# Gate and up products of two layers by seven half products

## The reference

```python
def modulate(x, g, shift, scale):
    return rmsnorm(x, g) * (1.0 + scale) + shift

def swiglu(h, wg, wu, wd):
    return (jax.nn.silu(h @ wg) * (h @ wu)) @ wd

x = x + g2 * swiglu(modulate(x, n_ffn, sh2, sc2), wg, wu, wd)
```

## Time and profile before

| | |
|---|---|
| time, median of 3 runs | 2484.01 us (2483.6 to 2484.45) |
| span of the profiled execution | 2480.8 us |
| its own time | not given apart; the median lies 3.2 us above the span |
| busy: TensorE, weight loads | 97%, 76% |
| busy: VectorE, ScalarE, GpSimd | 38%, 36%, 34% |
| layer 0's feed-forward | about 440 to 1000 us of the span |
| layer 1's feed-forward | about 1433 to 1797 us |

### The profile page before, as it was taken

One profiled execution on the slowest core, in us unless ns is written; L12 is line 12 of the kernel. 1 busy time (PEld: TensorE's weight loads), 2 busy tenths in 40 slices (PEclk: granted clock), 3 DMA queues, 4 the chain that ended last, 5 costly groups with the idle time before them and its releaser, 6 DMA issues.

```text
span 2480.8 us, 34754 instructions
## 1 busy us (share of the span) xinstructions
PE 2402.4 (97%) x13237; PEld 1892.2 (76%) x13237; DVE 941.1 (38%) x1440; ACT 887.4 (36%) x1690; POOL 852.9 (34%) x705
## 2 busy tenths in 40 slices
PE   6999999999999999899899999999999998999998
PEld 4776666788888888687577778888887656888887
DVE  5556632411111113555357331111527666422322
ACT  4336632321121122343556332222423564422331
POOL 1223002223323233352002345445644532444443
PEclk9999999999999999999899999999999999999999
DMA  8630027322222213421020243333333201333332
GB/s 268 187 111 10 2 90 239 89 67 60 62 65 59 68 53 108 122 68 37 7 44 18 86 120 100 93 101 94 103 93 79 80 1 35 94 102 94 98 98 76
DMA packets 336116, 209.76 MB, mean 85 GB/s; under 512 B 29315, under 2 KB 308588, under 8 KB 335986
## 3 DMA queue, kind: packets, MB, share of 16 engines
q1 hardware_dynamic: 333330, 201.98, 28.1%
q10 hardware_dynamic: 2592, 5.96, 0.7%
q0 software_dynamic: 64, 0.04, 0.0%
HBM read 205.82 MB, written 2.12 MB: 84 GB/s over the span
## 4 chain that ended last, share of the span: by engine, by line
PE 86%; DVE 4%; issue 4%; ACT 2%; DMA 1%; POOL 1%; SPq 0%; DVEq 0%; ACTq 0%; POOLq 0%
PE G L1670 22%; PE G L1671 21%; PE G L1672 21%; PE G L1889 5%; PE G L1917 4%; PE G L1902 4%; PE G L1754 1%; POOL wlo L961 1%; PE G L1861 1%; PE G L1935 1%; PE G L1694 1%; PE G L1712 1%; PE G L1695 1%; PE G L1696 1%; DVE ssq L2189 1%
## 5 line engine op out<-in xcount | busy, mean ns | idle before, releaser
L961 POOL TENSOR_TENSOR wlo<-raw,whi 128x512 fp32r<-128x512 f32 x564 | 745.9, 1344 | 1386.6 <-ACT whi L1155 1386.5
L1155 ACT ACTIVATE whi<-raw 128x512 fp32r<-128x512 f32 x564 | 325.4, 624 | 1199.8 <-PE G L1672 1081.4
L1670 PE MATMUL G<-big_a,whi 128*128 128x512 f32 x2016 | 740.3, 367 | 2.2 <-POOL wlo L961 1.5
L1671 PE MATMUL G<-big_a,wlo 128*128 128x512 f32 x2016 | 728.1, 361 | 0.0
L1672 PE MATMUL G<-big_a,whi 128*128 128x512 f32 x2016 | 724.5, 359 | 0.0
L1670 PEld LDWEIGHTS G<-big_a,whi 128*128 128x128 f32 x2016 | 379.9, 188 | 76.3 <-issue 12.6
L1671 PEld LDWEIGHTS G<-big_a,wlo 128*128 128x128 f32 x2016 | 379.8, 188 | 63.3 <-issue 6.7
L1672 PEld LDWEIGHTS G<-big_a,whi 128*128 128x128 f32 x2016 | 378.8, 188 | 60.2
L1670 PE MATMUL G<-big_b,whi 128*128 128x512 f32 x856 | 315.3, 368 | 0.9 <-issue 0.9
L1671 PE MATMUL G<-big_b,wlo 128*128 128x512 f32 x856 | 315.5, 369 | 0.0
L1672 PE MATMUL G<-big_b,whi 128*128 128x512 f32 x856 | 314.3, 367 | 0.0
(11 more groups left out here) (270 smaller groups left out, 2215.2 us busy)
## 6 DMA issues: line engine op xcount, KB each, us to landing
raw<-in_l_ada_w_dram SPq DMA_DIRECT2D x84, 512.0 KB, 4.8
raw<-in_l_ffn_w_gate_dram SPq DMA_DIRECT2D x44, 512.0 KB, 3.8
raw<-in_l_ffn_w_up_dram SPq DMA_DIRECT2D x44, 512.0 KB, 3.8
raw<-in_l_ffn_w_down_dram SPq DMA_DIRECT2D x32, 512.0 KB, 4.0
raw<-in_w_up_dram SPq DMA_DIRECT2D x32, 512.0 KB, 4.0
raw<-in_w_down_dram SPq DMA_DIRECT2D x32, 512.0 KB, 4.0
raw<-in_w_in_dram SPq DMA_DIRECT2D x28, 512.0 KB, 3.8
raw<-in_l_w_in_dram SPq DMA_DIRECT2D x24, 512.0 KB, 4.0
```

Source lines behind the costliest of these rows:

```text
L961: ins = pool.tensor_tensor(wlo[:, u % 2, k:k + 4], raw[:, r % RING, k:k + 4], whi[:, u % 2, k:k + 4].bitcast(F32), ALU.subtract)
L1155: act.activation(whi[:, u % 2, k:k + 4], raw[:, r % RING, k:k + 4], ACT.Copy).then_inc(hi_done, 1)
L1670: pe.matmul(o, whi[:, u % 2, k], rlo[:, k, t0:t0 + w], start=k == order[0], stop=False)
L1671: pe.matmul(o, wlo[:, u % 2, k], rhi[:, k, t0:t0 + w], start=False, stop=False)
```

## The change

With the weights of two output tiles and all input tiles seen as 2 x 2 blocks (input tiles even and odd, output tiles first and second), and the activations as 2 x 2 blocks (input tiles even and odd, tokens first and second half), the two tiles are formed by seven products of half size in place of eight (Winograd's form of Strassen's scheme). Each half product is 4 input tiles by three matmuls over half of the tokens: 384 columns in layer 0, 256 in layer 1.

```diff
+FFN_CHUNKS0 = [(0, 2)] + [(2 + f0, nf) for f0, nf in split_width(FFN // P - 2, 4)]
+LOW_WORDS = T + 2 * TX + 2 * T + 5 * T
...
             for c, (f0, nf) in enumerate(chunks):
-                for i in range(nf * (2 if gated else 1)):
+                plain = nf * (2 if gated else 1)
+                if l in FAST:
+                    plain = 4 if c == 0 else 0
+                for i in range(plain):
                     plan_unit(("up", l, c, i), r=rings[i] if c == 0 and i < len(rings) else None)
+                if l in FAST and nf > plain // 2:
+                    plan_section(l, c, plain // 2, nf - plain // 2)
...
+        FAST = (0,1)
+        CHUNKS = {0: FFN_CHUNKS0 if 0 in FAST else FFN_CHUNKS, 1: FFN_CHUNKS}
```

In both layers tiles 0 and 1 stay plain (4 units). The other 20 are made in sections: layer 0's chunks are now 2, 4, 4, 4, 4, 4 tiles, layer 1's stay 8, 8, 6. A section is a row of sets, gate and up in turn for each pair of tiles. TensorE's part:

```diff
+                for at, st in enumerate(sec["sets"]):
...
+                    for q in range(7):
+                        s = slot_of(sec, 7 * p + q)
+                        if q in (2, 3):
+                            pe.wait_ge(PH["fast", "lod"], 2 * p + q - 1)
+                        elif q >= 5:
+                            r = st["r"][q - 5]
+                            pe.wait_ge(raw_free[r % RING], r // RING + 1)
+                        else:
+                            pe.wait_ge(PH["fast", "lop"], 3 * p + (q + 1 if q < 2 else 3))
...
+                        for j in range(4):
...
+                            xhi, xlo = operands(q, j)
+                            pe.matmul(outs[q], half_slot(whi, s)[:, j], xlo, start=j == 0, stop=False)
+                            pe.matmul(outs[q], half_slot(wlo, s)[:, j], xhi, start=False, stop=False)
+                            mm = pe.matmul(outs[q], half_slot(whi, s)[:, j], xhi, start=False, stop=j == 3)
+                        mm.then_inc(done, 1)
```

`whi` and `wlo` are used as four half slots, so ScalarE can turn out the weights of half product i + 4 when i has finished (`fast_next`). The four sums of weight blocks (`fast_sum`) and the low parts of half products 2 and 3 (`fast_lower`) are VectorE's; the other five low parts are GpSimd's (`fast_lowers`). VectorE also combines the seven results out of PSUM and multiplies gate and up:

```diff
+                    for q in range(7):
+                        if q == 2:
+                            dve.wait_ge(done, 7 * p + 3)
+                            dve.wait_ge(PH["fast", "copy"], p + 1)
+                            dve.tensor_tensor(c[:, 0:2], b26, twice(s1), ALU.add).then_inc(out, 1)
+                        elif q == 4:
...
+                            dve.tensor_tensor(mid, b57, twice(c[:, 1]), ALU.add).then_inc(out, 1)
...
+                            dve.tensor_tensor(c[:, 3], b57[:, 1], mid[:, 0], ALU.add).then_inc(out, 1)
+                            if up:
...
+                                dve.tensor_tensor(c[:, 0::3], c[:, 0::3], sg[:, 0::3], ALU.mult).then_inc(mult, 1)
+                        elif q == 6:
...
+                            dve.tensor_tensor(c[:, 1:3], b34, mid, ALU.add).then_inc(out, 1)
...
+                        if ahead:
+                            if q in (2, 3):
+                                fast_sum(ahead, q - 2)
+                            elif q == 5:
+                                fast_sum(ahead, 2)
+                                fast_lower(sec, ahead, 2)
+                            elif q == 6:
+                                fast_lower(sec, ahead, 3)
+                                fast_sum(ahead, 3)
+                        if not up and at and q < 2:
+                            hidden_tile(sec["sets"][at - 1], q)
```

The activations need four sums too, for each half of the input tiles (`fast_operand_sums`, 8 operations, then 8 high parts on ScalarE and 8 low parts on VectorE). To form them the norm keeps the unrounded tile: ScalarE writes it (`full_row`) and rounds it by a second copy. In layer 1 the sums stand right behind the norm, ahead of the modulation columns; in layer 0 they stand behind them:

```diff
+                if l in FAST and l:
+                    fast_operand_sums(l)
                 if i in HOSTED:
                     ada_columns(*HOSTED[i][1])
```

More of the change, by code:

```diff
@@ L284, in build, with half_tiles, wslot @@
         plan = {}
-        cnt = {"r": 0, "u": 0, "g": 0, "a": 0}
+        cnt = {"r": 0, "u": 0, "g": 0, "a": 0, "p": 0, "pair": 0, "w4": None}
+        flips = []
+        narrow = {}
+        def half_tiles(u):
+            return narrow.get(u, 4)
+        def wslot(u):
+            return (u + sum(1 for first in flips if u >= first)) % 2
         ring_dmas = []
@@ L723, in build @@
         shared_sems(("ffn_act", "ffn_prod", "ffn_hi", "ffn_lo"),
-                    [(f"ffn{i}", (n // P,) * 4) for i, n in enumerate((FFN, FFN, FF2))])
+                    [(f"ffn{i}", ((2 if i in FAST else n // P),) * 2 + (n // P,) * 2)
+                     for i, n in enumerate((FFN, FFN, FF2))])
+        stage_sems("fast", "sum", "hi", "lop", "lod", "done", "copy", "out", "silu", "hid", "full", "tsum", "thi", "tlo")
+        flat_scr = scr[:].rearrange("p a b -> p (a b)")
+        W1, W2, W4 = (part(flat_scr, 3072 + 512 * i, 4, P) for i in range(3))
@@ L1113, in _ @@
                 lower(u)
[L1114 to L1115 removed]
+            for u in range(4):
+                lower(first["up", 0, 0, 0] + u)
+            fast_ffn(0, CHUNKS[0])
+            for u in range(first["down", 0, len(CHUNKS[0]) - 1, 0], first["in1"] + 6):
                 lower(u)
@@ new lines, in fast_ffn @@
+            def fast_ffn(l, chunks, ranges, h_ready):
+                for c, (f0, nf) in enumerate(chunks):
+                    if c == 0:
+                        first_units([("up", l, 0, 0), ("up", l, 0, 1)], lambda b: ranges, h_ready)
+                        ada_turn(*HOSTED[1 + 2 * l][1])
+                        for b in range(2, 4):
+                            unit(("up", l, 0, b), hhi, hlo, ranges)
+                    p = None
+                    if sets_of(l, c):
+                        fast_section(plan["sec", l, c])
+                        p = sets_of(l, c)[-1]["p"]
+                        pe.wait_ge(PH["fast", "copy"], p + 1)
+                    down_pair(l, c, nf, f0, ranges, p)
+                    groups = ADA_DOWN0 if l == 0 and c == len(chunks) - 1 else ()
+                    for b in range(1, KD):
+                        if b > 1:
+                            if p is not None and b < 4:
+                                pe.wait_ge(PH["fast", "out"], 4 * p + b + 1)
+                            unit(("down", l, c, b), ahi, alo, ranges, k_tiles=nf)
+                            if b <= len(groups) and groups[b - 1]:
+                                ada_turn(*groups[b - 1])
+                        if b < len(groups) and groups[b]:
+                            ada(*groups[b])
```

437 lines of the change are left out of this document (409 added, 28 removed).

## The result

The changed kernel takes 2455.02 us (median of 4 runs, 2453.43 to 2459.95), the kernel before beside it 2484.23 us (2483.6 to 2484.45): ratio 0.9886, 95% interval 0.9872 to 0.9900. The forecast was 2448, range 2428 to 2474: faster, as said, and 7 us less of it than said.

What follows compares the result with a forecast made beforehand. TensorE, busy 97% of the span, was taken as the bound. Layer 0's sets -44, layer 1's -4.6 and +13 on the path gave -35.6: span about 2445, forecast 2448 with 3.2 us median offset, range 2428 to 2474.

Steps and rivals of the forecast that it cites:

- Layer 0's sets: Layer 0 gate and up: 84 matmuls per tile pair at 0.174 us, 14.6 us, saving 44 us over 20 sets.
- The rival of weight loads: Weight loads of 0.188 us don't hide behind narrow matmuls; 15.8 us a set in both layers, 2575 us; chance 0.02.
- First chunk: Layer 0's first two-tile chunk: TensorE waits for VectorE's sums, conversions and the second hidden tile; 5 us, bounds 2 to 8.
- Five section ends in layer 0: Layer 0's five later chunks end with a 4.2 us chain against 4.2 us of input tiles; 0.3 each, 1.5 us.
- Modulation loads in the last chunk: Layer 0's last chunk: down units end closer together, so the fourth modulation load comes late; 2.5 us, bounds 0 to 4.
- Layer 1's sets: Layer 1 gate and up: VectorE, with waiting on GpSimd, becomes the bound at 10.65 us a set; 4.6 us saved over 20.
- the opening: Layer 1's first section waits for the first hidden tiles while VectorE carries extra sums and low parts; 2.5 us, 0 to 5.
- the signs named: Expected: layer 1 sets of 10.6 us, gaps before half products 2, 3 or 0 released by VectorE or GpSimd low parts.
- Down units in layer 1: Units 0 and 1 end 1.36 us apart but the third needs 0.62 + 1.27 us; 0.5 us a chunk, 1.5 in all.
- The norms: One more copy a tile (0.8 us) on ScalarE, its turn 2.1 us, hidden behind TensorE's 2.1 us a tile; no cost.
- the waiting stays hidden: Rival: layer 1's sets take TensorE's 10.1 us with no waiting showing, 2437 us; chance 0.19.
- The exclusion costs in full: Rival: VectorE and GpSimd SBUF operations exclude each other whole; layer 1 sets take 11.9 us, 2473 us; chance 0.17.

Runs made afterwards that it cites:

- experiment 5: Changed kernel with layer 0's first chunk reordered (second half of activation sums converted later, tile 0 of both down units first): 2450.62 us; with layer 0 alone by half products, 2449.72.
- experiment 6: Changed kernel with the modulation columns of layer 0's last chunk hosted between down units 4 and 5 instead of 1 and 2: 2453.65 us.
- Experiments 2: Changed kernel with product 3's low part on VectorE put ahead of the second multiply of the hidden tiles at an up set's end: 2454.31 us.
- experiment 4: Changed kernel with product 4's low part computed by VectorE instead of GpSimd, in both layers: 2445.11 us.
- experiment 3: Changed kernel, layer 1's sections: GpSimd's low parts computed for 8 of 128 columns only, 2437.65 us; or VectorE's sums, low parts and multiplies cut likewise, 2437.08 us.
- experiment 7: Changed kernel with down unit 1 doing only half its tiles ahead of unit 0's last two, so unit 0 ends earlier: 2452.3 us.
- the two cut kernels: Changed kernel with most columns left out in layer 1's sections, of GpSimd's low parts (2437.65 us) or of VectorE's sums, low parts and multiplies (2437.08 us).

## Why the prediction was right or wrong

- **Layer 0's sets**, -44 by 0.174 us a matmul: 0.173, and -45. Right, on the value read off the line between two sizes. The rival of weight loads is out.
- **First chunk**, 5 (2 to 8): 3.65 us at the down units (3.77 from start to start), 0.7 at one tile of the norm, 0.1 ahead of the first section, and then 2.5 us that no step had: TensorE ran at 1.2 GHz behind the wait and took 5.3 us, from 479.81 to 485.07, for 9 matmuls of 512 columns and 6 of 256, the work of 2.8 (0.43 us from start to start of 512 columns, 0.23 elsewhere). 6.9 in all. The mechanism was right (experiment 5); the clock was missed.
- **Five section ends in layer 0**, 1.5: 0.15 each over the 33.6 us of plain work, 0.7.
- **Modulation loads in the last chunk**, 2.5: from the product's first matmul to the next unit 4.9 us, 2.0 before, so 2.9, and 2.1 of it the wait for the fourth load (experiment 6). Not foreseen: the next four loads, hosted by the norm behind it, are late too (TensorE waits 2.2 us for the last), and from that product's first matmul to the norm's it takes 4.9 us, 3.6 before: 1.3 more. That both come from the shorter units is argued from the order of the loads, not shown by a run.
- **Layer 1's sets**, -4.6 with 10.65 us a set, and 2.5 for the opening: 10.82, and 3.0. This is the step that failed. The text made VectorE's average load the bound: 8.0 + 2.6 = 10.6. Its work was over-estimated and its waiting well estimated: 78.06 / 8 = 9.8 us a set, which is 7.2 of its own (57.5 / 8, with GpSimd cut; 8.0 forecast) and the 2.6 of waiting that was forecast; but with 9.8 VectorE is not the bound. That 10.65 lies so near 10.82 is in part luck: it came from a sum that bounds nothing here. Of the signs named, gaps came before half products 3 and 0, but before 1 and 6 too. What the average left out is the row of work in time: GpSimd's low parts of products 4, 5, 6, 0 and 1 come one behind the other, and where VectorE lengthens them to 1.7 us each TensorE, at 1.44 a product, follows GpSimd's pace; at product 3 it follows VectorE. And each wait has a price of its own, 0.05 and 0.10 us, that no step had: half of the 6.4 us. Experiments 2 and 3 show that the lateness comes from the two engines lengthening each other, not from the order or the hand-offs alone; experiment 4 agrees, by taking one low part out of GpSimd's row. The 0.46 us that a VectorE operation was said to cost GpSimd was what was left of the one in that row: the exclusion is full, both ways (experiment 3). An estimate from its rows: each GpSimd low part holds VectorE off for 1.15 us and each VectorE operation holds GpSimd off for 0.55, so 5 x 1.15 + 8 x 0.55 = 10.2 us of a set go one behind the other, as much as TensorE's 10.08, and 4 x 1.15 + 9 x 0.55 = 9.6 with one low part moved.
- **Down units in layer 1**, 0.5 a chunk: 1.1 to 1.2, 3.4 in all (experiment 7 shows size and cause). The two units end 1.36 us apart as forecast, but the third waits for a conversion, two hand-offs and 1.28 us of GpSimd, 2.2 us in all.
- **The norms**, 0: none in layer 1 (its first two units take 11.0 us, as before), and the 0.7 at one tile in layer 0.

Over the forecast, together: layer 1's sets and opening 3.9, its down units 1.9, the first chunk with the clock 1.9, the loads 0.4 and the hosted ones 1.3, the third layer 0.5, less 0.8 of the sets and 0.8 of the section ends in layer 0: 8.3 of the 9.5 us between the span of 2454.5 and the 2445 forecast. The last us isn't located. Of the rivals, *the waiting stays hidden* names what the two cut kernels show (2437 forecast for it, 2437 and 2438 measured, though by taking work away). *The exclusion costs in full* had the mechanism right and the price wrong: 11.9 us a set took 1.27 and 0.69 us for what 1.15 and 0.55 are.

What stays open: whether layer 1's sets reach 10.08 by moving more of GpSimd's work; the opening of layer 1's first section, where 1.5 us are left.

## What to carry to other kernels

Where two engines feed a third that has no slack, an average load below its own isn't enough: look at the longest row of work without a pause on each feeder, with its instructions as long as they are beside the other's, and add a fixed price for each wait. Then an operation that one engine does in half the other's time can be worth moving to that engine, even if it is the busier of the two, as here. Where units get shorter, look at everything that was hidden behind them, loads and conversions alike, and at each wait of 2 us or more on TensorE for what the clock adds.
